# Moving the vector copies, the gate copies and the PSUM banks of the pooling stage in a two-layer transformer trunk

## The chip, the cores and the metric

The kernel runs on one core of a Trainium2 chip. Five engines work side by side, each on its own list of instructions in order, and wait for each other only by semaphores: PE (TensorE, matmuls; its weight loads are shown apart as PEld), DVE (VectorE), ACT (ScalarE), POOL (GpSimd, nearly unused here) and SP (SyncE, which starts the DMA transfers). Matmul results land in PSUM, which has eight banks; ACT or DVE must read a bank before PE may overwrite it. The metric is the time of one execution on the device, in microseconds (us).

## The reference, cut to what matters

Two layers work on 256 context tokens and 256 latent tokens with 1024 features. The change lies in the mixer of layer 0, and in the vectors that modulate it:

```python
def adaln(cvec, w, b):                       # six vectors of 1024 from one conditioning vector
    m = jax.nn.silu(cvec) @ w + b
    return tuple(jnp.split(m[:, None, :], N_MOD, axis=-1))

def chunk_gmlp(a, v_gain, w_s, b_s):         # ya
    u, v = a[..., :A_WIDTH], a[..., A_WIDTH:]
    v = rmsnorm(v, v_gain)
    ...
    s = jnp.einsum('gpq,bcqgd->bcpgd', w_s, vc) + b_s.T[:, :, None]
    return u * s.reshape(b, l, A_WIDTH)

def ab_mixer(h, w_in, v_gain, w_s, b_s, w_pool, p_scale, w_out):
    z = h @ w_in                             # 1024 -> 1536: u, v, and 512 columns for pooling
    ya = chunk_gmlp(jax.nn.gelu(z[..., :2 * A_WIDTH], approximate=False), v_gain, w_s, b_s)
    yb = multiscale_pool(z[..., 2 * A_WIDTH:], w_pool, p_scale)   # centred means, then a 128x128 product per group
    return jnp.concatenate([ya, yb], axis=-1) @ w_out
```

After it come a SwiGLU layer, attention in layer 1, and a top-2-of-8 mixture of experts, which takes half of the time. None of these is edited.

## The kernel before, in words

Tokens are worked in four tiles of 128 (`t` = 0 to 3, two of context, two of latent tokens). Every weight comes as a slab of 128 x 2048 float32 (1 MB) into one of six `raw` buffers. ACT copies it to `hi` in a rounded format (L458, the function `split_hi`), DVE subtracts to get `lo` (L464, `split_lo`), and PE computes each product as three matmuls, hi by hi, hi by lo and lo by hi (L505 to L507). There are three pairs of `hi` and `lo`. PE cannot begin on a slab before its `lo` is written.

The modulation weights of blocks `cb` 4 to 9 take another way. `direct(0, cb, h)` multiplies and sums half a block on DVE (eight instructions at L1026), and `spread(0, cb)` on PE sums over the partitions. For blocks 4 and 5 (the residual gates) `spread` writes two full banks, 5 and 6 (L1517), one for each kind of token, and `gate(0, cb)` on ACT copies them to `gate_rows` (L667). For the other blocks it writes eight columns (L1523), and DVE copies them (L996). The six blocks are interleaved with the mixer's slabs by a list, `MIX_STEPS`.

The mixer's input projection `ab_in` has six slabs, `j` = 0 to 5, of 256 output columns. For each, PE makes four groups of 24 matmuls, one a token tile, in bank `(4j+t) % 5`. ACT takes the gelu of slabs 0 to 3 out of their banks into `u` and `v` (L726). Then it squares `v` (L734) and takes a root (L736), and DVE scales `v` (L1072, L1075). DVE copies slabs 4 and 5 into `zp` (L1067), which is what the pooling reads. After slabs 2 and 3 PE runs `spread(0, 4)` and `spread(0, 5)`.

Then four small stages follow. `ab_s` (L1585) multiplies `v` with the chunk matrices into banks 0 to 3. DVE adds a bias and multiplies with `u` (16 instructions, L1092). `ab_pool` (L1595) multiplies `zp` with a band matrix, one bank for each of four groups `g`, and DVE copies each out to `pooledT` (`pooled(g)`, L1081). `ab_yb` (L1601) multiplies it with the group's matrix, ACT scales that into `ybtmp` (L743), and DVE splits it into `Hhi` and `Hlo` (`yb(g)`, L940 and L942). PE issues these as pool 0, pool 1, yb 0, pool 2, yb 1, pool 3, yb 2, yb 3. Then it transposes `u` (`ab_ya`, L1611), which ACT and DVE split (L745, L1108), runs `spread(0, 6)` and `spread(0, 7)`, and begins the output projection `ab_out` (four slabs). DVE adds its results to the residual `X` (L976, L978).

The order on each engine is that of the Python code. Which bank a result uses stands in a table, `bank_order`: its entries are (key, bank) in the order in which PE uses them, and a bank's next use waits until the one listed before it has been emptied. The waits of PE, ACT and DVE on each other's results all come from this table.

Of the kernel before, what the change touches and what calls it, by code (L numbers as in the profile page):

```python
# [43 lines left out]
NT = 4  # L44
# [58 lines left out]
def bank_order():  # L103

    out = []

    out.append(("start", 1, [("cT", 0)]))
    for cb in range(4):
        out.append(("ada0", 1, [(("m", cb), 5 + cb % 2, (cb, 1)), (("col", cb), 7)]))
    out.append(("ada0", 1, [(("bc", cb, who), 5 + who) for cb in (4, 5) for who in range(2)]))  # L110
    out.append(("norm0", 1, [(k, k % 5) for k in range(8)]))
    out.append(("wsT", 1, [("wsT", 4)]))
    out.append(("ab_in", 1, [((j, t), (4 * j + t) % 5) + ((j,) if t == 3 else ()) for j in range(6) for t in range(NT)]))
    out.append(("ab_s", 1, [(t, t) for t in range(NT)]))
    for g in (0, 1, 2, 3, 4):
        out.append(("ab_pool", 1, [(g, 5 + g % 2)] if g < 4 else []))
        out.append(("ab_yb", 1, [(g - 1, 7 if g % 2 else 4)] if g >= 1 else []))
    out.append(("ada0", 1, [(("col", cb), b) for cb, b in ((6, 7), (7, 5), (8, 6), (9, 7))]))
    out.append(("ab_ya", 1, [(g, (3 + g) % 5) for g in range(4)]))
    out.append(("ab_out", 1, [((h, t), (4 * h + t) % 5) + (((h, 1),) if t == 3 else ()) for h in range(2) for t in range(NT)]))  # L120
    out.append(("norm1", 1, [(k, k % 5) for k in range(8)]))
# [108 lines left out]
def build(nc, a, out):  # L230
# [38 lines left out]
    with ExitStack() as ctx:  # L269
# [42 lines left out]
        zp = sb("zp", [P, NT, AW], into=free0)  # L312
# [7 lines left out]
        pooledT = v[:, 0:2, :]  # L320
# [164 lines left out]
        def full(eng, stage, key, it=0, lag=0):  # L485

            b, _, _, r, per, closing = banks[stage, key]
            if closing is None:
                eng.wait_ge(bank_full[b], r + 1 - lag * per + it * per)
            else:  # L490
                n0, per = slabs[stage, closing][:2]
                eng.wait_ge(slab_used, n0 + 1 - lag * per + it * per)
            return ps[b]

        def emptied(ins, stage, key):
            ins.then_inc(bank_emptied[banks[stage, key][0]], 1)

        def await_emptied(eng, stage, key, it=0, lag=0):

            b, r, per = banks[stage, key][:3]  # L500
            eng.wait_ge(bank_emptied[b], r + 1 - lag * per + it * per)
# [144 lines left out]
        def _(act):  # L646
# [5 lines left out]
            def splits(stage, *keys, it=0, size=SLAB):  # L652
                for key in keys:
                    split_hi(act, stage, key, size, it)
# [6 lines left out]
            def gate(layer, cb):  # L661

                st = f"ada{layer}"
                for who in range(2 - layer):
                    b = full(act, st, ("bc", cb, who))
                    rows = gates[who][:, cb // 6, :] if layer == 0 else gates1[:, 0, :] if cb < 6 else gateM[:]
                    emptied(nc.scalar.activation(rows[:, (cb % 2) * 512:(cb % 2 + 1) * 512], b[:], ACT.Copy), st, ("bc", cb, who))  # L667
# [48 lines left out]
            for j in range(6):  # L716
                if j < 5:
                    splits("ab_in", j + 1)
                else:
                    splits("ab_out", (0, 0), (0, 1))  # L720
                if j in (3, 4):
                    gate(0, 1 + j)
                if j < 4:
                    for t in range(NT):
                        dst = (u if j < 2 else v)[:, t, (j % 2) * 256:(j % 2 + 1) * 256]
                        emptied(nc.scalar.activation(dst, full(act, "ab_in", (j, t))[:, 0:256], ACT.Gelu), "ab_in", (j, t))  # L726
                if j == 3:
                    for t in range(NT):
                        await_emptied(act, "ab_in", (3, t))
                        if t:  # L730
                            act.wait_ge(sumsq[4], t)
                        else:
                            await_emptied(act, "wsT", "wsT")
                        nc.scalar.activation(vsq, v[:, t, :], ACT.Square, accum_out=ssq[:, t, 1:2]).then_inc(sumsq[4], 1)  # L734
                    act.wait_ge(meansq[4], 1)
                    nc.scalar.activation(root[:, :, 1:2], rstd[:, :, 1:2], ACT.Sqrt).then_inc(rooted[4], 1)  # L736
            splits("ab_out", (1, 0))
            act.wait_ge(ab_consts, 16 * 4)
            for g in range(4):
                b = full(act, "ab_yb", g)  # L740
# [82 lines left out]
            for i in range(34):  # L823
                if i < 32:
                    b = full(act, "att", ("s", i))
# [104 lines left out]
        def _(dve):  # L930
            chain = Count(dve, dve_chain)
            V = nc.vector

            def splits(stage, *keys, it=0, size=SLAB):
                for key in keys:
                    split_lo(dve, stage, key, size, it)

            def hi_lo(dst_hi, dst_lo, src, ready):

                chain.mark(V.tensor_copy(dst_hi, src))  # L940
                chain.wait()
                V.tensor_tensor(dst_lo, src, dst_hi.bitcast(F32), ALU.subtract).then_inc(ready, 1)  # L942
# [112 lines left out]
            emptied(V.tensor_copy(wsT[:], full(dve, "wsT", "wsT")[:]), "wsT", "wsT")  # L1055
            await_emptied(dve, "wsT", "wsT")
            for j in range(6):
                if j < 5:
                    splits("ab_in", j + 1)
                for cb, h in MIX_STEPS[j]:  # L1060
                    direct(0, cb, h)
                if j == 5:
                    splits("ab_out", (0, 0), (0, 1))
                if j >= 4:
                    for t in range(NT):
                        b = full(dve, "ab_in", (j, t))
                        emptied(V.tensor_copy(zp[:, t, (j - 4) * 256:(j - 3) * 256], b[:, 0:256]), "ab_in", (j, t))  # L1067
                if j == 3:

                    dve.wait_ge(sumsq[4], NT)  # L1070
                    inverse_root(4, [(rstd[:, :, 1:2], ssq[:, :, 1:2], AW)])
                    chain.mark(V.reciprocal(rstd[:, :, 1:2], root[:, :, 1:2]))  # L1072
                    chain.wait()
                    for t in range(NT):
                        V.scalar_tensor_tensor(out=v[:, t, :], in0=v[:, t, :], scalar=rstd[:, t, 1:2], in1=vgain[:],  # L1075
                                               op0=ALU.mult, op1=ALU.mult).then_inc(v_ready, 1)
            def pooled(g):
                b = full(dve, "ab_pool", g)
                if g >= 2:
                    full(dve, "ab_yb", g - 2)  # L1080
                emptied(V.tensor_copy(pooledT[:, g % 2, :], b[:]), "ab_pool", g)  # L1081

            await_emptied(dve, "ab_in", (5, 3))
            for t in range(NT):
                full(dve, "ab_s", t)
            pooled(0)
            pooled(1)
            for t in range(NT):
                b = full(dve, "ab_s", t)
                for g in range(4):  # L1090
# [4 lines left out]
                        chain.mark(ins)  # L1095
                emptied(ins, "ab_s", t)

            def yb(g):
                await_emptied(dve, "ab_yb", g)
                hi_lo(Hhi[:, 4 + g, :], Hlo[:, 4 + g, :], ybtmp[:, g % 2, :], y_ready)  # L1100
            for g in range(4):
                yb(g)
                if g < 2:
                    pooled(g + 2)
            for g in range(4):
                b = full(dve, "ab_ya", g)
                dve.wait_ge(ya_hi, g + 1)
# [840 lines left out]
```

## Time and profile before

| what | value |
|---|---|
| median of 3 runs | 1865.67 us (1865.26 to 1866.6) |
| the profiled execution | 1865.67 us, of which 1863.3 us are the span from first to last instruction |
| PE busy | 1724.8 us, 93% of the span |
| DVE busy | 1388.8 us, 75% |
| ACT busy | 920.4 us, 49% |
| mean granted TensorE clock | 0.939 of 2.4 GHz |

Times within the execution are counted from the start of the span. The stretch that the change touches is from 93 us (the end of slab 3's preparation) to 155 us (the first matmul of `ab_out`). A busy share is no measure of what could be gained; what counts is which wait ends last at each place.

### The profile page before, as it was taken

To read this page: it belongs to the slowest core of one execution; us is meant where nothing else is said; L and a number is where in the kernel's file an instruction comes from. 1 tells how busy PE (TensorE), PEld (TensorE's weight loads), DVE (VectorE), ACT (ScalarE), POOL (GpSimd) and SP (SyncE) were. 2 spreads that over 40 slices of the span, in tenths; PEclk is the share of its full clock that TensorE was granted. 3 is DMA by queue.
4 is the path that set the end of the run, shared out by engine and by line. 5 is a ranking of instruction groups with operands and counts; after the bars stand their busy time and mean duration, and the time that the engine had idled before them with its cause. 6 is when DMAs were issued, how large, how long until landed. Compare 5 with 4: busy or idle time off the path is not lost.

```text
span 1863.3 us, 22507 instructions
## 1 busy us (share of the span) xinstructions
PE 1724.8 (93%) x8417; PEld 1408.4 (76%) x8418; DVE 1388.8 (75%) x1442; ACT 920.4 (49%) x844; POOL 0.2 (0%) x4
## 2 busy tenths in 40 slices
PE   4999899999999777997699998999899998999995
PEld 1897687888887775666588886888788887888884
DVE  5889577677777556464497987888698977888886
ACT  5431412112111534122477776767677776767674
POOL 0000000000000000000000000000000000000000
PEclk9999899999999787579799999999999999999998
DMA  9563235445654222000299998999899998999992
GB/s 352 184 226 113 90 118 177 136 138 194 211 183 148 94 91 68 0 1 23 86 352 336 355 337 290 359 333 367 279 347 341 349 340 290 353 344 360 334 363 93
DMA packets 214552, 426.38 MB, mean 229 GB/s; under 512 B 8186, under 2 KB 64028, under 8 KB 214452
## 3 DMA queue, kind: packets, MB, share of 16 engines
q1 hardware_dynamic: 210218, 420.37, 64.8%
q10 hardware_dynamic: 4234, 4.57, 0.8%
q8 instruction: 76, 1.25, 0.3%
q14 instruction: 24, 0.20, 0.0%
HBM read 423.86 MB, written 1.05 MB: 228 GB/s over the span
## 4 chain that ended last, share of the span: by engine, by line
PE 87%; DVE 6%; ACT 2%; issue 2%; DMA 1%; SPq 1%; DVEq 0%; ACTq 0%
PE bank L505 25%; PE bank L506 25%; PE bank L507 25%; PE bank L1748 3%; PE bank L1737 2%; PE bank L1803 2%; DVE lo L464 2%; PE bank L1842 1%; PE bank L1754 1%; PE bank L1523 1%; DMA raw<-in_ada_w_dram 1%; DVE acc L1026 1%; ACT hi L458 1%; PE bank L1876 0%; PE bank L1877 0%
## 5 line engine op out<-in xcount | busy, mean ns | idle before, releaser
L464 DVE TENSOR_TENSOR lo<-raw,hi 128x2048 fp32r<-128x2048 f32 x361 | 820.7, 2282 | 221.8 <-ACT hi L458 219.9
L458 ACT ACTIVATE hi<-raw 128x2048 fp32r<-128x2048 f32 x361 | 689.1, 1911 | 476.4 <-PE bank L507 469.8
L506 PE MATMUL bank<-lo,xgh 128*128 128x512 f32 (+1 forms) x864 | 328.2, 380 | 14.7 <-issue 14.7
L505 PE MATMUL bank<-hi,xgh 128*128 128x512 f32 (+1 forms) x864 | 331.0, 383 | 8.6 <-DVE lo L464 6.3
L507 PE MATMUL bank<-hi,xgl 128*128 128x512 f32 (+1 forms) x864 | 327.5, 379 | 0.0
L506 PEld LDWEIGHTS bank<-lo,xgh 128*128 128x128 f32 x864 | 164.5, 190 | 47.4 <-issue 15.7
L505 PEld LDWEIGHTS bank<-hi,xgh 128*128 128x128 f32 x864 | 164.4, 190 | 42.0 <-DVE lo L464 6.5
L507 PEld LDWEIGHTS bank<-hi,xgl 128*128 128x128 f32 x864 | 164.4, 190 | 33.3
L505 PE MATMUL bank<-hi,aTh 128*128 128x512 f32 x396 | 159.1, 402 | 0.0
L507 PE MATMUL bank<-hi,aTl 128*128 128x512 f32 x396 | 154.8, 391 | 0.0
L506 PE MATMUL bank<-lo,aTh 128*128 128x512 f32 x396 | 154.3, 390 | 0.0
L1026 DVE SCALAR_TENSOR_TENSOR acc<-raw,cs,acc 128x512 f32<-128x512 f32 x216 | 146.6, 746 | 1.4
L505 PE MATMUL bank<-Hhi,hi 128*128 128x512 f32 x352 | 140.5, 399 | 2.8 <-issue 2.8
L507 PE MATMUL bank<-Hhi,lo 128*128 128x512 f32 x352 | 138.9, 395 | 0.0
L506 PE MATMUL bank<-Hlo,hi 128*128 128x512 f32 x352 | 138.5, 393 | 0.0
L507 PEld LDWEIGHTS bank<-hi,aTl 128*128 128x128 f32 x396 | 74.3, 188 | 16.6
L506 PEld LDWEIGHTS bank<-lo,aTh 128*128 128x128 f32 x396 | 74.6, 188 | 13.8
L505 PEld LDWEIGHTS bank<-hi,aTh 128*128 128x128 f32 x396 | 74.5, 188 | 13.6
L505 PE MATMUL bank<-hi,Hhi 128*128 128x256 f32 (+1 forms) x256 | 80.9, 316 | 0.0
L505 PEld LDWEIGHTS bank<-Hhi,hi 128*128 128x128 f32 x352 | 66.6, 189 | 17.8 <-issue 3.7
L507 PE MATMUL bank<-hi,Hlo 128*128 128x256 f32 (+1 forms) x256 | 79.6, 311 | 0.0
L506 PE MATMUL bank<-lo,Hhi 128*128 128x256 f32 (+1 forms) x256 | 79.6, 311 | 0.0
(316 smaller groups left out, 2249.6 us busy)
## 6 DMA issues: line engine op xcount, KB each, us to landing
raw<-in_moe_w_gate_dram SPq DMA_DIRECT2D x99, 1024.0 KB, 5.8
raw<-in_moe_w_up_dram SPq DMA_DIRECT2D x99, 1024.0 KB, 6.3
raw<-in_moe_w_down_dram SPq DMA_DIRECT2D x99, 1024.0 KB, 5.9
raw<-in_ada_w_dram SPq DMA_DIRECT2D x48, 1024.0 KB, 5.9
raw<-in_ffn_w_gate_dram SPq DMA_DIRECT2D x11, 1024.0 KB, 5.4
raw<-in_ffn_w_up_dram SPq DMA_DIRECT2D x11, 1024.0 KB, 5.5
raw<-in_ffn_w_down_dram SPq DMA_DIRECT2D x11, 1024.0 KB, 5.0
raw<-in_ab_w_in_dram SPq DMA_DIRECT2D x6, 1024.0 KB, 8.7
```

The lines of the kernel that those rows point to most:

```text
L458: nc.scalar.activation(hi[n0 % SPL][:, 0:size], raw[slot][:, 0:size], ACT.Copy).then_inc(hi_ready, 1)
L464: nc.vector.tensor_tensor(lo[n0 % SPL][:, 0:size], raw[slot][:, 0:size], hi[n0 % SPL][:, 0:size].bitcast(F32), ALU.subtract).then_inc(lo_r ...
L505: nc.tensor.matmul(dst, lh, rh, start=first, stop=False, skip_group_check=True)
L506: nc.tensor.matmul(dst, lh, rl, start=False, stop=False, skip_group_check=True)
L507: return nc.tensor.matmul(dst, ll, rh, start=False, stop=last, skip_group_check=True)
L1026: ins = V.scalar_tensor_tensor(out=sum_, in0=w_, scalar=c_, in1=biased[:, place_, :] if h == 0 and i < 2 else sum_, op0=ALU.mult, op1=ALU.add)
L1523: ins = T.matmul(b[:, 2 * j + who:2 * j + who + 1], sums[:, who, j * P:(j + 1) * P], ones[:, 0:1], start=True, stop=True)
L1737: filled(T.matmul(bank(pe, "att", ("s", i))[:], q_, k_, start=True, stop=True), "att", ("s", i))
L1748: ins = T.matmul(b[:, 0:64], pT[:, i % 2, t * P:(t + 1) * P], val, start=(t == 0), stop=(t == 3))
L1754: ins = T.transpose(b[:, t * P:(t + 1) * P], pexp[:, (i - 1) % 2, t * P:(t + 1) * P], ident[:])
L1803: ins = T.matmul(b[:, kk * P:(kk + 1) * P], src[:, t, k * P:(k + 1) * P], Pm[:, par, t, :], start=(t == 0), stop=(t == 1))
L1842: ins = T.transpose(b[:, j * P:(j + 1) * P], ame[:, c % 2, j * P:(j + 1) * P], ident[:])
```

## The change

Three things move, and the arithmetic stays the same.

1. On ACT the copies of the gate blocks, `gate(0, 4)` and `gate(0, 5)`, go from the front of steps `j` = 3 and 4 to their end. The first splits of `ab_out` are written after the loop.
2. On DVE the copies of slabs 4 and 5 into `zp` go to the front of their step, ahead of the split of the next slab and of the `direct` sums. The first two splits of `ab_out` go behind the loop, and the multiplications with `u` ahead of the first two `pooled` copies.
3. In the bank table pool and yb go from banks 4 to 7 to banks 0 to 4, and blocks 6 to 9 are listed earlier (with the banks that they had).

```diff
-    out.append(("ada0", 1, [(("bc", cb, who), 5 + who) for cb in (4, 5) for who in range(2)]))
+    out.append(("ada0", 1, [(("bc", cb, who), 5 + who) for cb in (4, 5) for who in range(2)] + [(("col", cb), b) for cb, b in ((6, 7), (7, 5), (8, 6), (9, 7))]))
...
-        out.append(("ab_pool", 1, [(g, 5 + g % 2)] if g < 4 else []))
-        out.append(("ab_yb", 1, [(g - 1, 7 if g % 2 else 4)] if g >= 1 else []))
+        out.append(("ab_pool", 1, [(g, g)] if g < 4 else []))
+        out.append(("ab_yb", 1, [(g - 1, (3 + g) % 5)] if g >= 1 else []))
...
# ACT, in the loop over j
                 if j < 5:
                     splits("ab_in", j + 1)
-                else:
-                    splits("ab_out", (0, 0), (0, 1))
-                if j in (3, 4):
-                    gate(0, 1 + j)
...
+                if j in (3, 4):
+                    gate(0, 1 + j)
-            splits("ab_out", (1, 0))
+            splits("ab_out", (0, 0), (0, 1), (1, 0))
...
# DVE, in the loop over j
+                if j >= 4:
+                    for t in range(NT):
+                        b = full(dve, "ab_in", (j, t))
+                        emptied(V.tensor_copy(zp[:, t, (j - 4) * 256:(j - 3) * 256], b[:, 0:256]), "ab_in", (j, t))
                 if j < 5:
                     splits("ab_in", j + 1)
                 for cb, h in MIX_STEPS[j]:
                     direct(0, cb, h)
-                if j == 5:
-                    splits("ab_out", (0, 0), (0, 1))
-                if j >= 4:
-                    for t in range(NT):
-                        ...
-            await_emptied(dve, "ab_in", (5, 3))
-            for t in range(NT):
-                full(dve, "ab_s", t)
-            pooled(0)
-            pooled(1)
+            splits("ab_out", (0, 0), (0, 1))
             for t in range(NT):
                 b = full(dve, "ab_s", t)
                 ...                                   # the 16 multiplications with u
+            pooled(0)
             for g in range(4):
+                if g < 3:
+                    pooled(g + 1)
                 yb(g)
-                if g < 2:
-                    pooled(g + 2)
```

How the instructions stand now at the three places that matter. First ACT from the split of slab 4 to the splits of `ab_out`, before (`gate_rows` are the gate copies, `v` the gelu of slab 3, `root` the root):

```order
L458 ACTIVATE hi<-raw 128x2048
L667 ACTIVATE gate_rows<-bank 128x512 x2
L726 ACTIVATE v<-bank 128x256 x4
L734 ACTIVATE zp,ssq<-v 128x512 x4
L736 ACT_TABLE_LOAD
L736 ACTIVATE root<-rstd 128x4
L458 ACTIVATE hi<-raw 128x2048
L667 ACTIVATE gate_rows<-bank 128x512 x2
L458 ACTIVATE hi<-raw 128x2048 x3
```

and in the changed kernel (its lines have other numbers, L666 is the gate copy):

```order
L457 ACTIVATE hi<-raw 128x2048
L721 ACTIVATE v<-bank 128x256 x4
L729 ACTIVATE zp,ssq<-v 128x512 x4
L731 ACT_TABLE_LOAD
L731 ACTIVATE root<-rstd 128x4
L666 ACTIVATE gate_rows<-bank 128x512 x2
L457 ACTIVATE hi<-raw 128x2048
L666 ACTIVATE gate_rows<-bank 128x512 x2
L457 ACTIVATE hi<-raw 128x2048 x3
```

The first pair of gate copies has moved behind the gelu, the squares and the root. Second, DVE from the scaling of `v` to the first split of yb, before (`zp` are the copies of slabs 4 and 5, `lo` the splits, `acc` the `direct` sums):

```order
L1075 SCALAR_TENSOR_TENSOR v<-v,rstd,vgain 128x512 x4
L464 TENSOR_TENSOR lo<-raw,hi 128x2048
L1026 SCALAR_TENSOR_TENSOR acc<-raw,cs,biased 128x512 x2
L1026 SCALAR_TENSOR_TENSOR acc<-raw,cs,acc 128x512 x6
L1067 COPY zp<-bank 128x256 x4
L1026 SCALAR_TENSOR_TENSOR acc<-raw,cs,acc 128x512 x8
L464 TENSOR_TENSOR lo<-raw,hi 128x2048 x2
L1067 COPY zp<-bank 128x256 x4
L1081 COPY v<-bank 128x512 x2
L1092 SCALAR_TENSOR_TENSOR u<-bank,pcols,u 128x128 x16
L940 CAST Hhi<-v 128x512
```

and now:

```order
L1070 SCALAR_TENSOR_TENSOR v<-v,rstd,vgain 128x512 x4
L1058 COPY zp<-bank 128x256 x4
L463 TENSOR_TENSOR lo<-raw,hi 128x2048
L1023 SCALAR_TENSOR_TENSOR acc<-raw,cs,biased 128x512 x2
L1023 SCALAR_TENSOR_TENSOR acc<-raw,cs,acc 128x512 x6
L1058 COPY zp<-bank 128x256 x4
L1023 SCALAR_TENSOR_TENSOR acc<-raw,cs,acc 128x512 x8
L463 TENSOR_TENSOR lo<-raw,hi 128x2048 x2
L1077 SCALAR_TENSOR_TENSOR u<-bank,pcols,u 128x128 x16
L1087 COPY v<-bank 128x512 x2
L937 CAST Hhi<-v 128x512
```

The copies of slab 4 stand ahead of the split of slab 5 (the `lo` row under them), those of slab 5 ahead of the last eight sums and two splits, and the multiplications ahead of the pooled copies. PE's list is the same in both; what differs is the banks. Third, PE on its pool (`band,zp`) and yb (`v,wpool`) matmuls with their waits, before:

```order
L1595 MATMUL bank5<-band,zp 128x144 [waits bank_emptied5,bank_emptied4]
L1595 MATMUL bank5<-band,zp 128x144 x3
L1595 MATMUL bank6<-band,zp 128x144 [waits bank_emptied6,bank_emptied4]
L1595 MATMUL bank6<-band,zp 128x144 x3
L1601 MATMUL bank7<-v,wpool 128x512 [waits bank_emptied7,bank_emptied5]
```

and now:

```order
L1587 MATMUL bank0<-band,zp 128x144 [waits bank_emptied0,bank_emptied4]
L1587 MATMUL bank0<-band,zp 128x144 x3
L1587 MATMUL bank1<-band,zp 128x144 [waits bank_emptied1,bank_emptied4]
L1587 MATMUL bank1<-band,zp 128x144 x3
L1593 MATMUL bank4<-v,wpool 128x512 [waits bank_emptied4,bank_emptied0]
```

Pool 0 now shares bank 0 with `ab_s` of tile 0, and pool 1 bank 1 with that of tile 1.

## Rows read from the trace of the kernel before

**Rows 1.** Chain of waits in the window 93 to 155 us: start, us, what.

```profile
112.19 2.20 DVE lo L464
...
126.32 4.40 DVE lo L464 x2
...
131.20 5.44 PE bank L1585 x32
```

**Rows 2.** Timeline of PE: start, us, engine, line, operation, tiles; idle time before it.

```profile
104.03 1.88 PE L1517 MATMUL bank<-acc,ones 128*128 128x512 f32 x4
...
105.87 0.28 PE L506 MATMUL bank<-lo,Hhi 128*128 128x256 f32 x1
...
117.06 0.28 PE L505 MATMUL bank<-hi,Hhi 128*128 128x256 f32 x1
...
131.20 5.44 PE L1585 MATMUL bank<-v,wsT 128*128 128x128 f32 x32 [2.67 <-DVE zp L1067]
136.48 2.13 PE L1595 MATMUL bank<-band,zp 128*128 128x144 f32 x16
138.51 1.12 PE L1601 MATMUL bank<-v,wpool 128*128 128x512 f32 x2
139.47 1.14 PE L1595 MATMUL bank<-band,zp 128*128 128x144 f32 x8
...
148.71 2.52 PE L1611 MATMUL bank<-ident,u 128*128 128x128 f32 x16
151.07 3.63 PE L1523 MATMUL bank<-ones,acc 128*128 128x1 f32 x32
154.56 0.48 PE L505 MATMUL bank<-hi,Hhi 128*128 128x512 f32 x1
```

**Rows 3.** Timeline of ACT, same columns.

```profile
93.29 1.08 ACT L667 ACTIVATE gate_rows<-bank 128x512 f32<-128x512 f32 x2
...
108.98 0.21 ACT L736 ACTIVATE root<-rstd 128x4 f32<-128x4 f32 x1
...
110.90 1.06 ACT L667 ACTIVATE gate_rows<-bank 128x512 f32<-128x512 f32 x2
...
128.63 1.91 ACT L458 ACTIVATE hi<-raw 128x2048 fp32r<-128x2048 f32 x1 [9.39 <-PE bank L507]
139.73 0.69 ACT L743 ACTIVATE v<-bank,pcols 128x512 f32<-128x512 f32 x1 [9.20 <-PE bank L1601]
```

**Rows 4.** Timeline of DVE, same columns.

```profile
119.61 1.41 DVE L1067 COPY zp<-bank 128x256 f32<-128x256 f32 x4
120.94 5.38 DVE L1026 SCALAR_TENSOR_TENSOR acc<-raw,cs,acc 128x512 f32<-128x512 f32 x8
...
130.64 1.42 DVE L1067 COPY zp<-bank 128x256 f32<-128x256 f32 x4
137.76 0.69 DVE L1081 COPY v<-bank 128x512 f32<-128x512 f32 x1 [5.71 <-PE bank L1595]
...
139.25 4.22 DVE L1092 SCALAR_TENSOR_TENSOR u<-bank,pcols,u 128x128 f32<-128x128 f32 x16
143.38 0.42 DVE L940 CAST Hhi<-v 128x512 fp32r<-128x512 f32 x1
143.84 0.69 DVE L942 TENSOR_TENSOR Hlo<-v,Hhi 128x512 fp32r<-128x512 f32 x1
```

**Rows 5.** Stretches: bounds, length, busy us of five engines, PEclk, DMA share, GB/s.

```profile
128.70:131.00 2.30, 0.00 (x0) 0.00 (x0) 2.30 (x3) 1.84 (x1) 0.00 (x0) 1.00 1.05 405
132.50:135.60 3.10, 3.10 (x17) 3.10 (x16) 0.00 (x0) 0.00 (x0) 0.00 (x0) 0.50 1.03 367
...
203.20:207.40 4.20, 0.00 (x0) 0.00 (x0) 3.10 (x8) 3.96 (x5) 0.00 (x0) 0.61 0.00 0
207.50:210.90 3.40, 3.38 (x16) 3.39 (x17) 3.40 (x2) 2.50 (x5) 0.00 (x0) 0.50 0.09 7
```

**Rows 6.** Timeline of DVE in the second half of ab_out.

```profile
193.02 0.69 DVE L976 TENSOR_TENSOR u<-bank,gate_rows 128x512 f32<-128x512 f32 x1 [6.63 <-PE bank L507]
```

More of the change, by code:

```diff
@@ L115, in bank_order @@
     for g in (0, 1, 2, 3, 4):
-        out.append(("ab_pool", 1, [(g, 5 + g % 2)] if g < 4 else []))
-        out.append(("ab_yb", 1, [(g - 1, 7 if g % 2 else 4)] if g >= 1 else []))
-    out.append(("ada0", 1, [(("col", cb), b) for cb, b in ((6, 7), (7, 5), (8, 6), (9, 7))]))
+        out.append(("ab_pool", 1, [(g, g)] if g < 4 else []))
+        out.append(("ab_yb", 1, [(g - 1, (3 + g) % 5)] if g >= 1 else []))
     out.append(("ab_ya", 1, [(g, (3 + g) % 5) for g in range(4)]))
@@ L1061, in _ @@
                     direct(0, cb, h)
-                if j == 5:
-                    splits("ab_out", (0, 0), (0, 1))
-                if j >= 4:
-                    for t in range(NT):
-                        b = full(dve, "ab_in", (j, t))
-                        emptied(V.tensor_copy(zp[:, t, (j - 4) * 256:(j - 3) * 256], b[:, 0:256]), "ab_in", (j, t))
                 if j == 3:
@@ L1076, in _ @@
                                                op0=ALU.mult, op1=ALU.mult).then_inc(v_ready, 1)
[L1077 to L1081, printed above, removed]
-            await_emptied(dve, "ab_in", (5, 3))
-            for t in range(NT):
-                full(dve, "ab_s", t)
-            pooled(0)
-            pooled(1)
+            splits("ab_out", (0, 0), (0, 1))
             for t in range(NT):
@@ L1096, in _, with pooled @@
                 emptied(ins, "ab_s", t)
+            def pooled(g):
+                b = full(dve, "ab_pool", g)
+                if g >= 2:
+                    full(dve, "ab_yb", g - 2)
+                emptied(V.tensor_copy(pooledT[:, g % 2, :], b[:]), "ab_pool", g)
             def yb(g):
```

## The prediction, made before the changed kernel ran

> **What bounds the kernel now.** I read the page first, then the chain of waits between 93 and 155 us, then the timelines of PE, ACT and DVE side by side for the same stretch, and last the granted clock of short stretches. Outside it no compute row moves, so what it gains or loses is carried to the end, unless a later wait absorbs it.
>
> In the chain of waits of the stretch the reader is to see that PE isn't what bounds it at first. From 112.19 us the chain runs over DVE: the split of slab 5, sums, and at 126.32 us two splits of `ab_out`. Only after the copies of slab 5 (130.64, 1.42 us) does PE begin `ab_s`, at 131.20 us [rows 1, 4]. PE had reached this point earlier: ACT is released by its last `ab_in` matmul at 128.63, and PE's row shows 2.67 us of idle time, ended by DVE's copy [rows 2, 3]. DVE then waits 5.71 us for the first pool product [rows 4]. These two waits are what the change can take away. From 139.25 us the multiplications, the short PE, ACT, DVE hops of yb and the transposes lead to the first `ab_out` matmul at 154.56 us [rows 2 to 4].
>
> **The gate copies on ACT.** Both pairs of `spread` write banks 5 and 6. So `spread(0, 5)`, which PE reaches at 104.03 us, needs the first pair emptied. Before, ACT emptied it at 93.29 us, ten microseconds early [rows 2, 3]. Now the pair stands behind the gelu, the squares and the root, whose row begins at 108.98 us and lasts 0.21. A pair takes 1.06 us, so its first half is done about 109.7 us. PE stands from 104.03 to 109.7: 5.7 us. Nothing hides it, as all of slab 4's matmuls are queued behind `spread(0, 5)`. ACT's root itself does not wait for PE, so there is no circle. The second pair needs nothing more: its results come after 110 us now, and its next reader is `ab_out`'s residual. ACT's hi of slab 5 is made about 1 us later, at 112 us, long before DVE wants it.
>
> **The copies on DVE, slab 4.** Their matmuls run from about 105.75 to 117.06 us, 0.1178 us apart [rows 2], now to 122.8. DVE is free at 112.19 and before took the split of slab 5 there (2.20 us) [rows 1]. Now it stands at the copies. Each waits for its tile, so the last is released when the last matmul of slab 4 is done, and only then comes the split, without which PE can't begin slab 5. The gap on PE is the last copy, a quarter of 1.41 us [rows 4], the split, 2.20 to 2.3, and two or three hand-overs of about 0.1: 2.9 us. Behind that split wait also the `direct` sums, but they have room beside slab 5's matmuls (11.2 us against 5.3).
>
> **From the end of slab 5 to `ab_out`.** Before, this takes 154.56 - 128.63 = 25.9 us [rows 2, 3]. Now DVE has after the last matmul: one copy 0.35, eight sums 5.3 (5.38 in its row), two splits 4.4, and the 16 multiplications 4.15: 14.2 us [rows 1, 4]. `ab_s` runs at once beside the sums, but pool 0 sits in bank 0 and must wait for the multiplications of tile 0, about 11 us after slab 5. It then is done beside the other tiles. Behind the multiplications nothing covers the hops any more. Counted from their end: pooled 0 copied at 0.6, yb 0 on PE at 0.7, ACT 1.2 us after it (138.51 to 139.73), its 0.69, a DVE pair of 0.42 and 0.69 to 3.8 [rows 2 to 4]; pooled 2 then to 4.4, yb 2 on PE at 4.6, pooled 3 at 6.1, yb 3 at 6.2, done at 7.1. Transposes and `spread(0, 6)`, `(0, 7)` took 5.85 us from 148.71 to 154.56, some of it at the low clock; 5.2 otherwise. That is 12.3, with 14.2 in all 26.5 us: 0.6 us more than before. So the 2.67 and the 5.71 us do go, but the sums and two splits that stood before the end of slab 5, beside its matmuls, now stand behind it.
>
> The Trainium skill (Perfetto Trace Analysis, section Optimizing Tensor Performance) says that independent matmul groups should rotate through different PSUM banks, so that the emptying of one runs beside the next group's matmuls. In this trace pool 0 ran in a bank of its own at 136.48, before the multiplications at 139.25 [rows 2, 4]. By that rule the new banks cost the beginning of pool 0, some 8 us later relative to slab 5's end; by the rows most of that lies beside DVE's own work, and my 0.6 us stays.
>
> **TensorE's clock.** After 2.67 us of idle time the stretch from 132.50 to 135.60 shows a granted clock of 0.50, that is 1.2 GHz, though PE is busy throughout; after 4.2 idle microseconds up to 207.40 the next 3.40 busy ones run at 0.50 too [rows 5]. At half clock PE loses half of such a stretch, 1.7 us. The wait of 5.7 us is longer than either, so I take 2.2 us behind it (none to 2.9: the low clock may come once or last longer, as slab 4 starts slowly). Behind the gap of 2.9 us I take 1.2 (none to 1.7). After `ab_s` PE idles some 8 us, and pool 0, pool 1 and yb 0 likely run at 1.2 GHz: pool and yb take about 1 us each at full clock (138.51, 139.47), so twice that; part of it lies beside the multiplications. I take 1.5 (none to 2.5).
>
> **Other edits.** The earlier listing of blocks 6 to 9 changes no wait: banks 5 to 7 are free from 113 us on. ab_out's first splits are late by some 10 us, but still end 15 us before its first matmul. The transfers that they free start later too: 1 MB takes 2.6 us at 405 GB/s [rows 5], and the four that are late are read first in `ab_out`, over 20 us on. Later DVE sums start when `ab_out` does, as before, with 6.63 us to spare in its second half [rows 6], so the shift goes through whole. In the experts' loop the lists lose a few register instructions (PE 3 of 101 rows, DVE 7 of 161); no row prices them, they are not where the big waits are, and I take 0, from -0.5 to +0.5.
>
> **The sum.** 5.7 + 2.9 + 0.6 = 9.2 us at full clock, and 2.2 + 1.2 + 1.5 = 4.9 us for the clock: 14.1 us slower. The profiled execution took 1865.67 us (span 1863.3), which is also the median, so 1879.8 us. With every clock term at nothing it is 1874.9, with all at their ends (7.1) 1882.0; one more for what the later stages' clock makes of the shift.
>
> **Rivals.**
> - The waits come as said, but PE keeps or regains the full clock: 1874.9 us. For it: in the stretch from 128.70 to 131.00 the clock still stood at 1.00 with PE idle, so it doesn't fall at once. Against it: both longer looks at such gaps end at 0.50 [rows 5].
> - The gate copies cost nothing, because PE has slack: it idled 2.67 us before `ab_s`, and DVE bounds the stretch. Then 2.9, 0.6 and the two later clock terms are left, 6.2 us: 1871.9 us. Against it: that slack was against a DVE that ran free of PE; now DVE's copies follow PE tile by tile, so a late PE makes DVE late.
> - Not slower: the copies leave the banks as they fill, `ab_s` starts at once and DVE never waits for pool 0. If nothing new stood before it, DVE's 5.7 us of waiting is the price: 1860.0 us. It decides if the first gate copy is done before 104.03 us and slab 5's `lo` before 117.06 us. The code's order speaks against both; I see only that I misread the bank table for it.
> - The Trainium skill (PSUM — Partial Sum Buffer, section Summary: rules for kernel authors) says to evacuate PSUM promptly. By it the earlier copies are the gain of the last rival; by the rows no matmul of slab 4 or 5 waited for its bank, so promptness buys only the 2.67 us.
> - The opposite end: the low clock holds over slab 4 and again over slab 5 and the yb hops, 1882.0 us and up.
>
> **Chances.** The forecast, both waits with some or all of the clock terms, 0.72; at full clock 0.12; beyond 1882 0.07; the gate wait hidden 0.04; not slower 0.05, of which 0.03 are faster. A change under 0.2% (3.7 us) can't be told from none for this kernel; of the rest only the last rival ends there. So faster 0.03, same 0.02, slower 0.95. The range goes from 1874.0 (the full-clock case and a microsecond) to 1883.0.
>
> **What would show it.** In the timeline of PE the first matmul of `spread(0, 5)` shows 5 to 6 us idle before it, released by ACT's `gate_rows` copy, and the first matmul of slab 5 shows about 2.9 us, released by DVE's `lo`. The 2.67 us before `ab_s` and DVE's 5.71 us at the first pooled copy are gone; PE is idle some 8 us before pool 0, released by the multiplications. PEclk falls to 0.50 behind the first wait, and within slab 4 the matmuls then start about twice as far apart as 0.1178 us. The first `ab_out` matmul comes at 168 to 169 us in place of 154.56, and from there on both timelines run in parallel. The prediction is wrong if PE passes `spread(0, 5)` at 104 us, or if the distance at `ab_out` is far from that at the end.

## The result, and the profile after

The changed kernel is slower by the amount forecast: 1878.88 us median of 4 runs (1876.95 to 1879.54) against 1865.47 for the kernel before (4 runs, 1863.88 to 1866.6), a ratio of 1.0070 with a 95% interval of 1.0053 to 1.0089. The forecast was 1879.8 us, the range 1874 to 1883.

| what | before | after |
|---|---|---|
| span of the profiled execution | 1863.3 us | 1876.4 us |
| PE reaches `spread(0, 5)` | 104.03 | 104.51 (110.13 less its 5.62 of waiting) |
| first `ab_out` matmul | 154.56 | 167.40 |
| between these two | 50.53 | 62.89 |
| from there to the end of the span | 1708.7 | 1709.0 |

So 12.4 of the 13.1 us of span arise between two points that are 50 us apart. What comes later takes the same time within 0.3 us, so it is shifted as a whole, though the distance between the two timelines wanders on the way (the section on the experiments says where). The stretch between the two points is my measure below, since it leaves out what varies elsewhere.

Here is who waited for whom between 93 and 170 us in the changed kernel (engine, line, releaser: us in total, times, longest). Its lines have other numbers: L1509 is `spread`, L504 to L506 the three products, L1587 pool, L1593 yb.

```profile
DVE zp L1058 <- PE bank L506: 17.8, 7, 4.6
...
PE bank L1587 <- DVE u L1077: 7.8, 1, 7.8
...
PE bank L1509 <- ACT gate_rows L666: 5.6, 1, 5.6
PEld bank L504 <- DVE lo L463: 2.9, 1, 2.9
PE bank L504 <- DVE lo L463: 2.7, 1, 2.7
```

The three PE waits are those that the prediction named. Weight loads (PEld) stand still with them. DVE, which never waited for slab 4 or 5 before, now waits 17.8 us for them. The timeline of PE shows where each falls; it answers to [rows 2]:

```profile
110.13 3.75 PE L1509 MATMUL bank<-acc,ones 128*128 128x512 f32 x4 [5.62 <-ACT gate_rows L666]
...
127.88 0.38 PE L504 MATMUL bank<-hi,Hhi 128*128 128x256 f32 x1 [2.72 <-DVE lo L463]
...
140.49 3.73 PE L1577 MATMUL bank<-v,wsT 128*128 128x128 f32 x32
151.99 3.94 PE L1587 MATMUL bank<-band,zp 128*128 128x144 f32 x16 [7.78 <-DVE u L1077]
...
161.20 1.12 PE L1593 MATMUL bank<-v,wpool 128*128 128x512 f32 x2 [0.65 <-DVE v L1087]
162.16 1.91 PE L1603 MATMUL bank<-ident,u 128*128 128x128 f32 x16
163.91 3.63 PE L1515 MATMUL bank<-ones,acc 128*128 128x1 f32 x32
167.40 0.48 PE L504 MATMUL bank<-hi,Hhi 128*128 128x512 f32 x1
```

`ab_s` now starts without idle time at 140.49, where before it showed 2.67 us, and takes 3.73 us in place of 5.44. The two engines that hold PE up are ACT and DVE. ACT's timeline shows the root and the gate copies straight behind it, against 93.29 before [rows 3]:

```profile
109.30 0.21 ACT L731 ACTIVATE root<-rstd 128x4 f32<-128x4 f32 x1
109.41 1.07 ACT L666 ACTIVATE gate_rows<-bank 128x512 f32<-128x512 f32 x2
```

DVE's timeline shows the copies of slab 4 spaced by PE, and the split of slab 5 behind the last; then, behind the last copy of slab 5 at 140.68, the sums, splits and multiplications, and the pooled copies (to be compared with [rows 4]):

```profile
117.05 0.43 DVE L1058 COPY zp<-bank 128x256 f32<-128x256 f32 x1 [4.55 <-PE bank L506]
...
125.20 0.42 DVE L1058 COPY zp<-bank 128x256 f32<-128x256 f32 x1 [2.29 <-PE bank L506]
125.55 2.28 DVE L463 TENSOR_TENSOR lo<-raw,hi 128x2048 fp32r<-128x2048 f32 x1
...
140.68 0.42 DVE L1058 COPY zp<-bank 128x256 f32<-128x256 f32 x1 [2.30 <-PE bank L506]
141.03 5.38 DVE L1023 SCALAR_TENSOR_TENSOR acc<-raw,cs,acc 128x512 f32<-128x512 f32 x8
146.32 4.48 DVE L463 TENSOR_TENSOR lo<-raw,hi 128x2048 fp32r<-128x2048 f32 x2
150.73 4.22 DVE L1077 SCALAR_TENSOR_TENSOR u<-bank,pcols,u 128x128 f32<-128x128 f32 x16
154.87 0.68 DVE L1087 COPY v<-bank 128x512 f32<-128x512 f32 x1
155.97 0.69 DVE L1087 COPY v<-bank 128x512 f32<-128x512 f32 x1 [0.43 <-PE bank L1587]
...
205.86 0.69 DVE L973 TENSOR_TENSOR u<-bank,gate_rows 128x512 f32<-128x512 f32 x1 [6.63 <-PE bank L506]
```

The last row answers to [rows 6]: its 6.63 us are the same, 12.84 us later. Last the granted clock, in stretches as in [rows 5] (PEclk is the third number from the end):

```profile
110.10:113.90 3.80, 3.77 (x6) 1.72 (x7) 2.39 (x4) 2.71 (x3) 0.00 (x0) 0.50 1.05 401
115.00:127.00 12.00, 10.17 (x90) 9.97 (x88) 3.07 (x5) 3.06 (x2) 0.00 (x0) 1.00 0.01 1
128.50:131.50 3.00, 3.00 (x16) 3.00 (x16) 3.00 (x5) 0.00 (x0) 0.00 (x0) 0.50 0.00 0
...
152.00:155.50 3.50, 3.50 (x15) 3.50 (x16) 3.50 (x13) 0.00 (x0) 0.00 (x0) 0.50 1.04 386
156.00:167.00 11.00, 10.35 (x69) 8.05 (x67) 8.81 (x16) 4.70 (x8) 0.00 (x0) 1.00 0.02 9
```

Each of the three waits is followed by 3.4 to 4.4 us of PE work at 1.2 GHz. The third such stretch lies on pool 0 and 1 and is over when yb begins at 155.77.

### The profile page after: what moved, and what is told of

It reads as the page before. It is cut to its first block, busy times and chain, and to the rows that moved or that the text cites. A ratio compares the mean times of both kernels' runs of the same rounds, so it can differ in the third digit from the quotient of the medians.

```text
span 1876.4 us, 22480 instructions
## 1 busy us (share of the span) xinstructions
PE 1727.8 (92%) x8417; PEld 1411.2 (75%) x8418; DVE 1389.2 (74%) x1442; ACT 920.6 (49%) x844; POOL 0.2 (0%) x4
## 3 DMA queue, kind: packets, MB, share of 16 engines
HBM read 423.86 MB, written 1.05 MB: 226 GB/s over the span
## 4 chain that ended last, share of the span: by engine, by line
PE 88%; DVE 6%; ACT 2%; issue 2%; DMA 1%; SPq 1%; DVEq 0%; ACTq 0%
PE bank L504 25%; PE bank L506 25%; PE bank L505 25%; PE bank L1740 2%; PE bank L1729 2%; PE bank L1795 2%; DVE lo L463 2%; PE bank L1834 1%; PE bank L1746 1%; PE bank L1515 1%; DMA raw<-in_ada_w_dram 1%; PE bank L1509 1%; ACT hi L457 1%; PE bank L1868 0%; PE bank L1869 0%
## 5 line engine op out<-in xcount | busy, mean ns | idle before, releaser
L504 PE MATMUL bank<-hi,xgh 128*128 128x512 f32 (+1 forms) x864 | 331.2, 383 | 8.8 <-DVE lo L463 6.3
L506 PE MATMUL bank<-hi,xgl 128*128 128x512 f32 (+1 forms) x864 | 327.8, 379 | 0.0
L504 PEld LDWEIGHTS bank<-hi,xgh 128*128 128x128 f32 x864 | 164.7, 191 | 42.3 <-DVE lo L463 6.5
L506 PEld LDWEIGHTS bank<-hi,xgl 128*128 128x128 f32 x864 | 164.5, 190 | 33.3
L504 PE MATMUL bank<-hi,aTh 128*128 128x512 f32 x396 | 159.1, 402 | 0.0
L506 PE MATMUL bank<-hi,aTl 128*128 128x512 f32 x396 | 154.8, 391 | 0.0
L504 PE MATMUL bank<-Hhi,hi 128*128 128x512 f32 x352 | 140.6, 399 | 2.8 <-issue 2.8
L506 PE MATMUL bank<-Hhi,lo 128*128 128x512 f32 x352 | 139.4, 396 | 0.0
L506 PEld LDWEIGHTS bank<-hi,aTl 128*128 128x128 f32 x396 | 74.3, 188 | 16.6
L504 PE MATMUL bank<-hi,Hhi 128*128 128x256 f32 (+1 forms) x256 | 82.5, 322 | 2.7 <-DVE lo L463 2.7
L504 PEld LDWEIGHTS bank<-hi,aTh 128*128 128x128 f32 x396 | 74.5, 188 | 13.6
L506 PE MATMUL bank<-hi,Hlo 128*128 128x256 f32 (+1 forms) x256 | 80.8, 316 | 0.0
L504 PEld LDWEIGHTS bank<-Hhi,hi 128*128 128x128 f32 x352 | 66.7, 189 | 18.0 <-issue 3.7
```

Source lines behind the costliest of these rows:

```text
L504: nc.tensor.matmul(dst, lh, rh, start=first, stop=False, skip_group_check=True)
L506: return nc.tensor.matmul(dst, ll, rh, start=False, stop=last, skip_group_check=True)
```

## The experiments

My theory was the sum of the prediction. The rivals were that the gate wait is hidden by DVE's lead, that prompt copies are a gain, and that the shared banks are the main cost. Eleven kernels were run. In the table "stretch" is the time from PE's arrival at `spread(0, 5)` to the first `ab_out` matmul in the one profiled execution, less 50.53 us. The medians stand beside those of the kernel before on the same chip. The runs were made on several chips, so below "in the medians" always means the difference to that kernel before, 13.4 us for the change. The last column is the time that the first half of `ab_out` takes, from its first matmul to the first one of its second half; its instructions are the same in all kernels.

| run | what it is | median (before) | ratio, 95% | stretch | half `ab_out` |
|---|---|---|---|---|---|
| before | | | | 0 | 24.2 |
| the change | | 1878.88 (1865.47) | 1.0053 to 1.0089 | +12.4 | 24.2 |
| e1 | before, gate copies moved | 1868.04 (1864.49) | 1.0010 to 1.0028 | +3.9 | 25.7 |
| e2 | before, DVE copies moved | 1869.78 (1864.49) | 1.0027 to 1.0051 | +2.4 | 25.6 |
| e3 | before, tail and banks moved | 1861.67 (1864.49) | 0.9979 to 1.0000 | -3.9 | 26.8 |
| e4 | change, gate copies back | 1868.80 (1864.49) | 1.0015 to 1.0037 | +5.2 | 24.2 |
| e5 | change, gate copies half way | 1871.71 (1863.96) | 1.0023 to 1.0045 | +7.1 | 26.4 |
| e6 | change, slab 5's split first | 1876.43 (1863.96) | 1.0049 to 1.0077 | +9.3 | 26.4 |
| e7 | change, old banks | 1880.61 (1863.96) | 1.0070 to 1.0097 | +14.8 | 27.0 |
| e8 | before, tail, one split later | 1860.00 (1863.96) | 0.9965 to 0.9988 | -3.7 | 25.7 |
| e9 | change, both waits away | 1866.79 (1864.60) | 0.9995 to 1.0018 | +2.3 | 26.6 |
| e10 | before, tail, old banks | 1861.44 (1864.60) | 0.9967 to 0.9989 | -2.9 | 26.4 |
| e11 | as e8, pooled copies earlier | 1857.92 (1864.60) | 0.9940 to 0.9967 | -6.9 | 25.7 |

The part behind the first `ab_out` matmul takes 1707.7 to 1710.8 us in most profiles, but 1705.7 in that of e4 and 1713.0 in that of e3, though their code is the same there. The stretch leaves this out, and with it two places where the clock differs between the profiles. One is the beginning of `ab_out`, just behind the stretch. PE runs there at full clock in before, the change and e4, and partly at 1.2 GHz in the ten others, though no idle time of more than 0.7 us stands in the 5 us ahead of it. It costs 1.4 to 2.8 us. First e6, then before:

```profile
163.70:170.30 6.60, 6.60 (x21) 5.60 (x21) 4.80 (x10) 0.00 (x0) 0.00 (x0) 0.50 0.01 4
154.60:159.40 4.80, 4.80 (x22) 3.90 (x23) 4.67 (x8) 0.00 (x0) 0.00 (x0) 1.00 0.00 2
```

The other is the attention of layer 1: from 800 to 818 us in before PE stays slow for longer than in the change, and the distance between the two falls from 15.3 us to 9.7 there and then grows again to 13.1. Each kernel has one kept profile, so how often its other executions look like it is not known. Where stretch and medians differ, both are given.

**e1, the gate copies alone.**

```diff
-                if j in (3, 4):
-                    gate(0, 1 + j)
                 if j < 4:                     # gelu
...
+                if j in (3, 4):
+                    gate(0, 1 + j)
```

> The kernel before with the move of the gate copies on ACT alone. Theory (two new waits on PE, of which the first is spread(0, 5) waiting for banks 5 and 6): PE stands 5.6 us before its spread; slab 4 then ends near 125 us, DVE meets its copies late, ab_s begins near 136.5 instead of 131.2, and the kernel is 4 to 7 us slower, about 1870.7 us. Rival (the wait lies in the slack that PE had against DVE, 2.67 us before ab_s): 3 us slower or less.

Measured: 3.6 us in the medians, 3.9 in the stretch. That is under my band of 4 to 7 and over the rival's 3, so the time alone decides for neither. The timeline of PE:

```profile
109.21 3.75 PE L1515 MATMUL bank<-acc,ones 128*128 128x512 f32 x4 [5.62 <-ACT gate_rows L667]
...
136.37 3.73 PE L1583 MATMUL bank<-v,wsT 128*128 128x128 f32 x32
```

The wait is 5.62 us, as in the whole change, and the low clock behind it costs another 2.8 us by the end of slab 5 (27.2 us from the start of `spread`, against 24.3 before). Of these 8.4 us the idle gap before `ab_s` (2.67 us in its row, 2.8 with the hand-over) hides 2.8, since PE is now the later one, and 5.6 are left: `ab_s` begins 32.8 us after PE's arrival in place of 27.2. So the slack hid its own length and no more. With the gap goes the low clock that `ab_s` had: 3.73 us in place of 5.44. That gave back 1.7 us, which my expectation had left out.

**e2, the slab copies alone** (the copies ahead of the split, and the `ab_out` splits behind the loop, as in the change's diff).

> The kernel before with the move of the slab 4 and 5 copies to the front of their step on DVE alone, and the two ab_out splits behind the loop; pooled copies still ahead of the multiplications, old banks. Theory: PE stands 2.9 us before slab 5 for its lo, the last sums and two splits come behind slab 5, and part of that is given back because DVE no longer waits 5.7 us for pool 0: about 4.3 us slower (2 to 6), 1869.8 us. Rival (prompt emptying is a gain, since the idle time before ab_s goes): not slower than before.

Measured: 5.3 us in the medians, 2.4 in the stretch; slower by both, and the rival falls. PE in its timeline has the 2.71 us before slab 5, and the pools long done when yb 0 starts:

```profile
120.06 0.38 PE L505 MATMUL bank<-hi,Hhi 128*128 128x256 f32 x1 [2.71 <-DVE lo L464]
...
134.63 2.13 PE L1594 MATMUL bank<-band,zp 128*128 128x144 f32 x16
142.05 2.08 PE L1600 MATMUL bank<-v,wpool 128*128 128x512 f32 x2 [5.29 <-DVE v L1080]
```

In this profile the clock stays full behind the gap of 2.71 us, where the change had 3.4 us at 1.2 GHz behind the same gap:

```profile
120.20:123.60 3.40, 3.40 (x31) 3.40 (x32) 3.40 (x6) 0.00 (x0) 0.00 (x0) 1.00 0.00 0
```

So this stretch lacks 1.7 us that a low clock there would cost, which may be part of why it is so much smaller than the difference of the medians.

**e3, the tail alone** (the multiplications ahead of `pooled(0)`, and the new banks).

> The kernel before with the end of the change alone: multiplications with u ahead of the pooled copies, and pool and yb in banks 0 to 4. Theory: on their own these edits are no loss; DVE multiplies while ab_s still runs instead of waiting 5.7 us for pool 0, so the first ab_out matmul comes about 4.5 us earlier (2 to 6), 1861 us. Rival (sharing banks 0 to 3 with ab_s is what costs, since pool must wait for the multiplications): slower than before by 1 to 8 us.

Measured: 2.8 us faster in the medians (the interval reaches to no change), 3.9 in the stretch. DVE's row now begins to multiply 0.32 us after its copies, while `ab_s` still runs; before, it waited 5.71 us there:

```profile
129.76 1.41 DVE L1067 COPY zp<-bank 128x256 f32<-128x256 f32 x4
131.49 1.13 DVE L1087 SCALAR_TENSOR_TENSOR u<-bank,pcols,u 128x128 f32<-128x128 f32 x4 [0.32 <-PE bank L1581]
```

This part of the change is good on its own. The single parts add up to 2.4 us in the stretch (3.9 + 2.4 - 3.9), the whole costs 12.4: they do not add. e1 and e2 both use up the gap before `ab_s` (2.8 us, and 1.7 for the low clock of `ab_s`), and e2 and e3 both DVE's 5.7 us at pool 0; in the whole change each can be used only once. With them the parts come to 12.6 us, an estimate from these rows.

**e4, the change with the gate copies back** (the reverse of e1's diff).

> The changed kernel with the gate copies on ACT put back ahead of the gelu. Theory: the 5.6 us wait before spread(0, 5) goes, and with it the low clock behind it that cost spread and the first matmuls 1.3 to 1.7 us; about 7 us faster than the changed kernel, 1872 us, still 6 us slower than before. Rival (the DVE order alone explains the loss, the gate wait is hidden by it): within 2 us of the changed kernel's 1878.9.

Measured: 7.2 us less than the change in the stretch, 9.1 in the medians. The gate wait costs its full length and more once DVE follows PE, and the rival falls.

**e5, a smaller dose.**

```diff
+                if j == 3:                    # behind the gelu
+                    gate(0, 4)
                 if j == 3:                    # squares and root
...
-                if j in (3, 4):
-                    gate(0, 1 + j)
+                if j == 4:
+                    gate(0, 5)
```

> The changed kernel with the first gate copies between the gelu and the squares instead of behind the root: a smaller dose of the same wait. Theory: PE then waits about 1 us before spread(0, 5) instead of 5.6, the clock does not fall behind it, and all but 1 us of what putting the copies back gave is there: 6 us faster than the changed kernel (5 to 7). Rival (what costs is that the copies come after the split of slab 4 and late at all, or the clock's phase): less than 3 us faster.

Measured: 5.7 us under the change in the medians, 5.3 in the stretch, as forecast, and the rival falls. The waits of PE:

```profile
PE bank L1511 <- ACT gate_rows L666: 1.1, 1, 1.1
```

It fell from 5.6 to 1.1 us, and `spread` took 1.96 us in place of 3.75: no low clock behind the short wait. So the position on ACT acts through this wait and its length.

**e6, the split of slab 5 first.**

```diff
+                if j < 5:
+                    splits("ab_in", j + 1)
                 if j >= 4:                    # copies into zp
...
-                if j < 5:
-                    splits("ab_in", j + 1)
```

> The changed kernel with the split of slab 5 put ahead of the copies of slab 4 on DVE (and nothing else moved but the split). Theory: the 2.7 us before slab 5 on PE go, with the low clock behind them (up to 1.7): 3 to 4.5 us faster than the changed kernel, 1874.5 to 1876 us. Rival (DVE's tail after slab 5 sets the end, and swallows it): within 1 us of the changed kernel. It would be swallowed if DVE, not PE's last slab 5 matmul, released the sums behind the copies.

Measured: 3.1 us under the change in the stretch, at the lower end of the theory, but 0.9 in the medians, where the rival stands (the intervals of the two differences to before, 9.1 to 14.4 us and 9.9 to 16.6, overlap widely). PE shows no wait before slab 5, so the wait does go with the order. What that is worth is not settled. In this profile the low clock on the beginning of `ab_out`, shown above, takes 2.2 of the 3.1 us back; the change has none there. e9 against e4, the same edit without the gate wait, gives 2.9 us in the stretch and 2.1 in the medians.

**e7, the old banks.**

```diff
-        out.append(("ab_pool", 1, [(g, g)] if g < 4 else []))
-        out.append(("ab_yb", 1, [(g - 1, (3 + g) % 5)] if g >= 1 else []))
+        out.append(("ab_pool", 1, [(g, 5 + g % 2)] if g < 4 else []))
+        out.append(("ab_yb", 1, [(g - 1, 7 if g % 2 else 4)] if g >= 1 else []))
```

The listing of blocks 6 to 9 went back to its old place too (not shown).

> The changed kernel with pool and yb in banks 4 to 7 as before. Theory: pool 0 and 1 run right behind ab_s and no longer stand 7.8 us for the multiplications, but their copies stand behind the multiplications anyway; only the low clock during pool 0 and 1 goes, which delayed the pooled copies by 0.4 us and yb 0 by a little: 0.5 to 1.5 us faster than the changed kernel. Rival (banks shared with ab_s are a main cost): 4 us faster or more.

Both were wrong: it is slower than the change, by 2.4 us in the stretch and 3.2 in the medians (whose intervals, 13.0 to 18.1 us and 9.9 to 16.6, overlap). PE, and the clock behind its gap:

```profile
143.56 2.13 PE L1588 MATMUL bank<-band,zp 128*128 128x144 f32 x16
155.11 2.08 PE L1594 MATMUL bank<-v,wpool 128*128 128x512 f32 x2 [9.42 <-DVE v L1088]
156.98 1.86 PE L1588 MATMUL bank<-band,zp 128*128 128x144 f32 x8
...
163.22 0.60 PE L1604 MATMUL bank<-ident,u 128*128 128x128 f32 x4
164.17 1.53 PE L1604 MATMUL bank<-ident,u 128*128 128x128 f32 x12 [0.34 <-ACT v L741]
```

```profile
155.10:158.40 3.30, 3.29 (x8) 2.26 (x9) 0.95 (x2) 0.69 (x1) 0.00 (x0) 0.50 0.25 94
```

The pools run early, as expected, but then nothing is left for PE while DVE multiplies. Its first work behind the gap is yb 0, on which ACT and DVE wait, and that runs at 1.2 GHz. ACT gets it late, and DVE stands idle 2.35 us for it:

```profile
158.00 0.43 DVE L938 CAST Hhi<-v 128x512 fp32r<-128x512 f32 x1 [2.35 <-ACT v L741]
```

From the start of yb 0 to the transposes 8.1 us pass, against 6.4 in the change, where the slow stretch fell on the pools: that is 1.7 of the 2.4 us. Another 0.6 has nothing to do with the clock. With the old banks the second group of transposes uses bank 4, which yb 3 used last, and waits for ACT to empty it (the row with 0.34), so that the transposes take 2.3 us in place of 1.75. The new banks spare them that. The rest is low clock at the end of `spread`. So the shared banks cost a wait, but in the better place, and they free another.

**e8, a candidate**: e10 with `splits("ab_out", (0, 1))` moved behind the slab 5 copies.

> The kernel before with the multiplications ahead of the pooled copies, old banks, and only one ab_out split ahead of the slab 5 copies on DVE, the other behind them. Theory: the copies end 0.6 us after slab 5's last matmul, so ab_s begins 2.2 us earlier and without the low clock behind an idle gap; the multiplications end near 135.5 us and the first ab_out matmul comes near 147.7 instead of 154.6: 6 to 7 us faster than before, 1858 us. Rival (something later takes the gain, as a fixed-time load or a clock phase): under 3 us faster.

Measured: 4.0 us faster in the medians, 3.7 in the stretch, between the theory's 6 to 7 and the rival's 3. `ab_s` does start at once (0.47 us of idle time), but the gap has moved to yb 0, and behind it pool 2 and yb 1 are slow:

```profile
136.28 1.13 PE L1598 MATMUL bank<-v,wpool 128*128 128x512 f32 x2 [2.06 <-DVE v L1082]
137.24 1.99 PE L1592 MATMUL bank<-band,zp 128*128 128x144 f32 x8
139.02 1.90 PE L1598 MATMUL bank<-v,wpool 128*128 128x512 f32 x2
```

**e9, both new waits away** (e4 and e6 together).

> The changed kernel with both new waits taken away: the gate copies back ahead of the gelu, and the split of slab 5 ahead of the copies of slab 4. What is left of the change is the last eight sums and two splits behind the slab 5 copies, the multiplications first, and the new banks. Theory (my term of 0.6 us for the stretch behind slab 5, plus up to 1.5 for its clock): 0.5 to 2.5 us slower than before, 1866 us. Rival (work moved behind slab 5 costs what it takes, less the two waits that go: 10.1 us of sums, splits and copy less 2.1 and 5.7): 3 us slower or more.

Measured: 2.2 us slower than before in the medians, with an interval that reaches to no change, and 2.3 in the stretch, within the theory's band. But theory and rival are not told apart: the interval also reaches to 3.4 us, and the rival's own sum, 10.1 less 2.1 and 5.7, is 2.3 and not 3 or more, as I wrote. The reason in that sum fits what was measured: the work that moved behind slab 5 costs little because the idle times that went pay for most of it.

**e10, the tail with the old banks** (e3 without its bank lines).

> The kernel before with the multiplications ahead of the pooled copies and nothing else; banks as before. Theory (in the changed kernel the new banks helped by about 2 us only because the low clock behind the idle gap fell on pool 0 and 1, which nobody waited for, and not on yb): here no long gap stands behind ab_s, so the same as with the new banks, 3 to 4 us faster than before, 1861 us. Rival (the new banks are themselves the gain): the same time as before.

Measured: 3.2 us faster in the medians, 2.9 in the stretch; e3 had 2.8 and 3.9. The order on DVE is the gain. What the banks add is at most the 1.0 us between the two stretches, of which 0.6 is the transposes' wait for bank 4 that e7 shows too.

**e11, the candidate again with the pooled copies in between.**

```diff
+            mults(0)
+            mults(1)
+            for t in (2, 3):
+                full(dve, "ab_s", t)
+            pooled(0)
+            pooled(1)
+            mults(2)
+            mults(3)
```

> The kernel before with one ab_out split behind the slab 5 copies, and the first two pooled copies in the middle of the 16 multiplications, so that the last eight cover the hops of yb 0. Theory: ab_s begins 2.2 us earlier as in the last candidate, and PE has no gap over 1 us before yb 0, so the low clock misses yb; the first ab_out matmul comes near 147 instead of 150.3: 6 to 7.5 us faster than before, 1857.5 us. Rival (the clock falls on another part of the chain, whatever the order): 4 us faster, as the last candidate.

Measured: 6.7 us faster than before in the medians, 6.9 in the stretch, and 20 us faster than the change. PE has no gap over 0.6 us, and every yb is quick:

```profile
128.14 3.81 PE L1589 MATMUL bank<-v,wsT 128*128 128x128 f32 x32 [0.47 <-DVE zp L1067]
...
133.90 1.12 PE L1605 MATMUL bank<-v,wpool 128*128 128x512 f32 x2
...
138.41 1.12 PE L1605 MATMUL bank<-v,wpool 128*128 128x512 f32 x2 [0.57 <-DVE v L1082]
140.08 1.12 PE L1605 MATMUL bank<-v,wpool 128*128 128x512 f32 x2 [0.54 <-DVE v L1082]
```

This is the version to keep: 1857.92 us, ratio 0.9940 to 0.9967. It too has the low clock on the beginning of `ab_out`, for 1.5 us, so it may not be the end.

## Why the prediction was right

Term by term, by the stretch of the profiled execution. Where a slab's end is needed, it is the start of its last matmul plus one pace: 125.0 for slab 4 and 140.5 for slab 5 after, 117.06 and 128.4 before.

| term | forecast | measured |
|---|---|---|
| wait before `spread(0, 5)` | 5.7 | 5.62 |
| low clock behind it, to the end of slab 4 | 2.2 | 1.8 (14.9 from 110.13 to 125.0, against 13.0) |
| gap before slab 5 | 2.9 | 2.9 (2.72 in PE's row) |
| low clock behind it, in slab 5 | 1.2 | 1.3 (12.6 against 11.3) |
| from the end of slab 5 to `ab_out` | 0.6 + 1.5 | 0.7 (26.9 against 26.2) |
| sum | 14.1 | 12.4 |

- The gate wait: its place, its releaser and its size were right. e4 and e5 show that it is the cause of more than half of the loss, and e1 that PE's slack hides no more than its own length of it; in the whole change even that is not there, since DVE's earlier copies had already closed the gap.
- The low clock behind it cost what was forecast, 2.2 us (4.4 us of work at half clock). The term shows 1.8 because the rest of slab 4 then ran 0.4 us faster than before (last section).
- The gap before slab 5: right, and e6 shows that it goes with the order alone. That the 2.9 and 1.3 us come back when it goes is not shown: e6 gave 3.1 us in the stretch and 0.9 in the medians, e9 against e4 2.9 and 2.1.
- The tail: the 0.6 us at full clock was right, and so was the main reason. Two idle times went, and sums and splits moved into the open; e9, with only this part left, is 2 us slower than before. One number in it was right for a wrong reason. I let transposes and `spread` shrink from 5.85 to 5.2 us because they would be at full clock. They took 5.24, but 0.6 of that gain came from the new banks, by which the transposes no longer wait for ACT (e7).
- The clock in the tail was the term that was mis-sized: 1.5 us forecast, about 0.1 measured. The low clock did come, but on pool 0 and 1, for which only the second pooled copy waited, 0.43 us. e7 shows what I had feared, with the low clock on yb: 1.7 us. Mainly for this reason the first `ab_out` matmul came at 167.4 us and not at 168 to 169.
- From the rivals, "full clock" (1874.9 us) is refuted by the clock rows, "gate wait hidden" by e4, "not slower" by all of the change's runs. Of the rule on rotating banks from the Trainium skill (Perfetto Trace Analysis, section Optimizing Tensor Performance), the wait that it warns of is there, 7.78 us before pool 0; but e7, which gives the pools banks of their own again, is not faster, so the measurement decides against it for the pools in this order of work. For the transposes the trace agrees with it: on a bank that was not just used they are 0.6 us shorter. The other rule of the Trainium skill, prompt evacuation (PSUM — Partial Sum Buffer, section Summary: rules for kernel authors), bought the 2.67 us and cost 2.9 by what was queued behind it, as the rows of e2 show.

What stays open: the medians of e2 and e6 lie 3 us further from before than their stretches do. In their profiles 1.4 and 2.2 us of that are the low clock on the beginning of `ab_out`, and e2 had none behind its gap. But e1, e9 and e10 have the same low clock on `ab_out`, and their medians agree with the stretch. What sets the clock at that place, no run was made to find, and single executions of the kernel before vary by 4 us and more.

## What to carry to other kernels

On an engine that works in order, an early read of a result bank is not early if the result isn't there: it blocks what stands behind it, and the price is the time of that (here the split of the next slab, 2.3 us). Before moving a copy back, look up the bank's next use, not the copied data's next reader: in the change the gate rows were first read over 70 us after they were copied, their bank was wanted at once. And where two idle times lie in one chain, moves that each remove one don't add up; test them together, and look for the order that leaves none, as e11 did.

## What the runs showed that I had not expected

- Where the low clock falls matters as much as whether it comes. The same 3.4 us or so at 1.2 GHz behind a gap of 8 to 9 us cost next to nothing on the pools (the change) and 1.7 us on yb (e7). The pools that waited were better placed than the pools that ran at once and left PE without work.
- A gap of 1.05 us before `spread` left the clock at full speed for it (e5, 1.96 us for four matmul rows), one of 5.62 us did not (3.75 us). Gaps of 2.7 us were followed by low clock in before, e4, e5 and the change, but the one before slab 5 in e2 was not. So the length of a gap alone does not tell.
- At the full granted clock the matmuls of a slab start 0.1178 us apart in some slabs and 0.1133 in others: slab 4 took the first pace before and the second after. That gave the change about 0.4 us back in slab 4. No run was made to find the cause.
